# One decoder step with grouped experts: from pairs of tiles to a pipeline of single tiles, with seven pairs' rows picked by the tensor engine from on-chip tokens

## What is computed

```python
def _hier_moe(x, w_group, b_group, w_expert, b_expert, w1, w3, w2):
    ...
    global_idx = g_idx * EXPERTS_PER_GROUP + e_idx
    combine = jnp.sum(jax.nn.one_hot(global_idx, N_EXPERTS, dtype=jnp.float32)
                      * gate[..., None], axis=1)
    ...
    for e in range(N_EXPERTS):
        hdn = jax.nn.silu(xf @ w1[e]) * (xf @ w3[e])
        acc = acc + combine[:, e:e + 1] * (hdn @ w2[e])
    return acc.reshape(bsz, T, d)

# layer:  x = LN1(alpha * x + mixer);  f = hier_moe(x);  x = LN2(alpha * x + f)
```

## Time and profile before

| what | us |
|---|---|
| device time, median of 3 runs (lowest, highest) | 725.46 (722.87, 726.48) |
| device time of the profiled execution | 724.48 |
| span of its trace, from the first to the last instruction | 722.7 |
| PE busy | 609.7 (84%) |
| DVE busy | 306.5 (42%) |
| ACT busy | 181.7 (25%) |
| POOL busy | 158.3 (22%) |

### The profile page before, as it was taken

The page is one execution under the profiler, slowest core; times in us unless marked ns, Lnnn a source line. Parts: engine busy times, 40 slices in busy tenths (PEclk is TensorE's granted clock), DMA queues, the critical chain, the costliest instruction groups (busy, mean ns, idle before and its releaser), DMA issues.

```text
span 722.7 us, 10598 instructions
## 1 busy us (share of the span) xinstructions
PE 609.7 (84%) x4220; PEld 419.2 (58%) x4220; DVE 306.5 (42%) x786; ACT 181.7 (25%) x287; POOL 158.3 (22%) x181
## 2 busy tenths in 40 slices
PE   5999999999899899799799798987777776877852
PEld 5999999878765356456445445544443534444430
DVE  4561585426584134344434343353426232323532
ACT  4232323201211223232332232223223222313210
POOL 1000000000000413343323234234132322224231
PEclk9999999999899999999999989999999999999996
DMA  9943033842668799999999999999999999999930
GB/s 268 282 159 133 2 117 117 350 189 103 246 293 349 285 418 420 418 417 416 422 415 419 414 423 417 421 418 417 422 417 424 414 426 416 424 419 416 391 135 8
DMA packets 45754, 235.99 MB, mean 327 GB/s; under 512 B 13683, under 2 KB 18291, under 8 KB 28728
## 3 DMA queue, kind: packets, MB, share of 16 engines
q1 hardware_dynamic: 32303, 220.92, 75.3%
q0 software_dynamic: 12544, 11.71, 4.8%
q10 hardware_dynamic: 857, 2.67, 0.9%
HBM read 237.69 MB, written 30.20 MB: 371 GB/s over the span
## 4 chain that ended last, share of the span: by engine, by line
issue 36%; SPq 18%; DMA 17%; PE 16%; POOL 9%; DVE 2%; ACT 1%; POOLq 0%; DVEq 0%
SPq L403 12%; DMA tenth_block<-in_w 12%; PE ps L543 9%; SPq L407 5%; PE ps L702 3%; DMA prev<-first_outputs,final_row 2%; POOL out L1094 2%; POOL first_outputs L1082 2%; POOL out L1090 2%; POOL prev L1086 2%; PE ps L723 2%; DMA first_outputs<-ye,first_row 2%; SPq L453 1%; DMA xe_odd<-x_rows,pair_row 1%; PE ps L506 1%
## 5 line engine op out<-in xcount | busy, mean ns | idle before, releaser
L702 PE MATMUL ps<-blocks,ln 128*64 128x256 f32 x1952 | 229.3, 391 | 54.4 <-DMA blocks<-in_w 38.7
L702 PEld LDWEIGHTS ps<-blocks,ln 128*64 128x64 f32 x1952 | 154.5, 140 | 128.6 <-issue 61.8
L723 PE MATMUL ps<-blocks,hT 128*64 128x512 f32 x464 | 109.9, 617 | 9.6 <-DMA blocks<-in_w 8.8
L1086 POOL DMA_INDIRECT prev<-first_outputs,final_row x32 | 34.4, 1076 | 234.3 <-DMA first_outputs<-ye_more,first_row 110.6
L723 PEld LDWEIGHTS ps<-blocks,hT 128*64 128x64 f32 x464 | 33.5, 141 | 68.0 <-issue 53.5
L807 ACT ACTIVATE ln<-ps 128x512 f32<-128x512 f32 (+1 forms) x38 | 20.0, 572 | 113.1 <-PE ps L690 94.2
L1496 DVE COPY hT<-ps 128x256 f32<-128x256 f32 x33 | 13.9, 421 | 71.3 <-PE ps L711 71.3
L543 PE MATMUL ps<-xT_high,w_in_high 128*128 128x288 f32 x256 | 40.6, 300 | 2.9 <-ACT w_in_high L807 1.7
L990 ACT ACTIVATE std<-rstd,eps 128x1 f32<-128x1 f32 x32 | 9.4, 295 | 123.9 <-DVEq L1523 114.3
L948 ACT ACTIVATE silu<-ps 128x256 f32<-128x256 f32 x33 | 12.7, 384 | 109.9 <-PE ps L702 105.3
L1491 DVE SCALAR_TENSOR_TENSOR h_rows<-silu,slot_gate,ps 128x256 f32<-128x256 f32 x33 | 15.7, 477 | 57.7 <-PE ps L702 57.6
(11 more groups left out here) (233 smaller groups left out, 787.4 us busy)
## 6 DMA issues: line engine op xcount, KB each, us to landing
blocks<-in_w SPq DMA_DIRECT2D x86, 2048.0 KB
tenth_block<-in_w SPq DMA_DIRECT2D x9, 2048.0 KB
blocks<-in_w_in SPq DMA_DIRECT2D x3, 2048.0 KB, 10.8
blocks<-in_w_out SPq DMA_DIRECT2D x2, 2048.0 KB, 7.9
x_tok<-in_x_prompt SPq DMA_DIRECT2D x4, 512.0 KB, 5.2
blocks<-in_w_in SPq DMA_DIRECT2D x4, 512.0 KB, 10.6
first_outputs<-in_x_prompt SPq DMA_DIRECT2D x4, 512.0 KB, 8.6
x_rows<-x_tok ACTq DMA_DIRECT2D x4, 512.0 KB, 2.7
```

What stands on the lines that cost most here:

```text
L702: mm = pe.matmul(ps[64 * g:64 * g + 64, bank, 0:FH], x, w[:, k, g * FH:(g + 1) * FH], start=(k == 0), stop=(k == KD - 1))
L723: mm = pe.matmul(ps[64 * g:64 * g + 64, BY, :], hT[:, k % 2, k // 2 * SLOTS:(k // 2 + 1) * SLOTS], w[:, k, g * DH:(g + 1) * DH], start=(k ...
L1086: return g.indirect_dma_start(out=prev[w], out_offset=None, in_=first_rows[:, :], in_offset=rows_at(idx), bounds_check=last_row, oob_is_er ...
```

## The change

- **PE runs single tiles**, one down behind: for tile t w1 t, turn t-1, w3 t, down t-1. The last tiles (30 to 32) do their own turn and down at once (`STAGGERED`).
- **The order of the loads** follows: w1 t, w3 t, w2 t-1. There are nine blocks, used in turn; the tenth is gone, since `x_tok` is still read.
- **Seven pairs are picked on chip**: for m = 3, 5, ..., 15 (`PICKED`) DVE makes a 0/1 matrix (`make_hot`) and PE multiplies it with `x_tok` (`pick_pair`, 10 products of 512 columns); ACT copies the result to `xe_odd` (`keep_xe`). The other nine are fetched as before.
- **POOL's loop** over t becomes `send(t-2)`, `load(t-1)`, `store(t-1)`, and `fetch` only where the pair isn't picked.
- **DVE's loop** becomes `final(t-2)`, `keep_hT(t-1)`, `products(t)`, `add_y(t-1)`, and `make_hot`.
- **ACT's loop** becomes `spread(t-2)`, `silu_of(t)`, and after odd t the copies and fills.
- **The start**: the token table is computed before the second `fetch_first`, `order` is made before the other index tables, the filler products on PE (`keep_warm`) are 21 in another place and 2 instead of 12.

```diff
+STAGGERED = E - 2
 def order_of_loads():
...
-    for m in range(1, PAIRS):
-        tiles = [t for t in (2 * m, 2 * m + 1) if t != SHARED + 1]
-        loads += [(kind, t) for t in tiles for kind in ("w1", "w3")] + [("w2", t) for t in tiles]
+    for t in range(E + 1):
+        loads += [(kind, t) for kind in ("w1", "w3")]
+        loads += [("w2", s) for s in ([t - 1] if t < STAGGERED else [t - 1, t] if t == STAGGERED else [t]) if s >= 0]
+    return [(kind, t) for kind, t in loads if t != SHARED + 1]
...
+HOME = [n % EARLY_BLOCKS for n in range(len(LOADS))]
+PICKED = list(range(3, PAIRS, 2))
...
             def block_free(n):
...
+                kind, t = LOADS[n - EARLY_BLOCKS]
+                sp.wait_ge({"w1": h1_done, "w3": h_done, "w2": y_done}[kind], t + 2 if t == SHARED else t + 1)
...
+            for n in range(EARLY_BLOCKS, EARLY_BLOCKS + 2):
+                block_free(n)
+                load(n)
+            sp.wait_ge(order_ready, 1)
+            for n in range(EARLY_BLOCKS + 2, EARLY_BLOCKS + 4):
...
-            keep_warm(21)
+            pe.wait_ge(out_kept, NT + 3)
+            keep_warm(4)
+            route(NT - 2)
+            turn_x1(NT - 1)
+            keep_warm(2)
+            route(NT - 1)
+            keep_warm(15)
...
+            def pick_pair(m):
+                n = PICKED.index(m)
+                pe.wait_ge(hot_ready, n + 3)
+                pe.wait_ge(xe_kept, 2 * n + 2)
+                pe.wait_ge(y_filled, 2)
+                for g in range(2):
+                    for j in range(NT):
+                        mm = pe.matmul(ps[:, BX[g], :], hot[:, j, :], x_tok[:, j, g * DH:(g + 1) * DH],
+                                       start=(j == 0), stop=(j == NT - 1))
+                    mm.then_inc(fetched, 1)
...
-            def first_pair():
+            def first_tiles():
...
+                token_table()
+                fetch_first(1, lambda: turn_hidden(0))
+                down(*place("w2", 0), 0, lambda: turn_first(1))
                 pe.wait_ge(xeT_ready, 2)
+                into_hidden("w1", *place("w1", 1), 1, 1)
+                into_hidden("w3", *place("w3", 1), 1, 1)
+                pe.wait_ge(table_ready, 1)
                 turn_pair(1)
...
-            def pair(m):
-                a, b = 2 * m, 2 * m + 1
-                pe.wait_ge(xeT_ready, 2 * m + 2)
-                into_hidden("w1", *place("w1", a), a, 0)
-                into_hidden("w3", *place("w3", a), a, 0)
-                into_hidden("w1", *place("w1", b), b, 1)
-                turn_hidden(a)
-                into_hidden("w3", *place("w3", b), b, 1)
-                down(*place("w2", a), a)
-                turn_hidden(b)
-                turn_pair(m + 1)
-                down(*place("w2", b), b)
+            def tile(t):
+                if t % 2 == 0:
+                    pe.wait_ge(xeT_ready, t + 2)
+                into_hidden("w1", *place("w1", t), t, t % 2)
+                if t <= STAGGERED:
+                    turn_hidden(t - 1)
+                into_hidden("w3", *place("w3", t), t, t % 2)
+                if t % 2:
+                    turn_pair((t + 1) // 2)
+                if t <= STAGGERED:
+                    down(*place("w2", t - 1), t - 1)
+                if t % 2 == 0 and (t + 2) // 2 in PICKED:
+                    pick_pair((t + 2) // 2)
...
-            keep_warm(12)
+            keep_warm(2)
+            first_tiles()
+            for t in range(2, E + 1):
+                tile(t)
+                if t >= STAGGERED:
+                    turn_hidden(t)
+                    down(*place("w2", t), t, last_half if t == E else None)
...
+            for t in range(2, E):
+                if t % 2 and (t + 1) // 2 in PICKED:
+                    keep_xe((t + 1) // 2)
+                if t > 2:
+                    spread(t - 2)
+                silu_of(t)
+                if t % 2:
+                    keep_xeT((t + 1) // 2)
+                    fill_pair((t + 1) // 2)
+            spread(E - 2)
+            spread(E - 1)
             silu_of(E)
-            spread(E - 1)
             spread(E)
...
-            g.memset(cleared[:, :], 0.0).then_inc(prev_cleared, 1)
+            g.memset(xe_odd[:, :, :], 0.0).then_inc(prev_cleared, 1)
             pool.wait_ge(prev_cleared, 1)
             pool.wait_ge(x1_stored, 16 * NT)
             fetch(1)
+            g.memset(prev_mem[:, :, :], 0.0).then_inc(prev_cleared, 1)
+            fetch(2)
             pool.wait_ge(first_cleared, 16 * NT)
             store(0)
-            load(1)
-            fetch(2)
-            store(1)
-            load(2)
-            for t in range(2, E - 1):
-                store(t)
-                send(t - 1)
-                if t < E - 2:
-                    load(t + 1)
-                if t % 2 == 0 and t // 2 + 2 <= PAIRS:
+            pool.wait_ge(prev_cleared, 2)
+            for t in range(2, E):
+                if t > 2:
+                    send(t - 2)
+                load(t - 1)
+                store(t - 1)
+                if t % 2 == 0 and t // 2 + 2 <= PAIRS and t // 2 + 2 not in PICKED:
                     fetch(t // 2 + 2)
+            load(E - 1)
             store(E - 1)
-            load(E - 1)
             send(E - 2)
             load(E)
...
+            def make_hot(m):
+                dve.wait_ge(fetched, 2 * PICKED.index(m) + 2)
+                for i in range(2):
+                    slot, one = pick_at[:, 2 + i, :], pick_at[:, 4, i * NT:(i + 1) * NT]
+                    settled(v.scalar_tensor_tensor(slot, pick_at[:, 0, :], float(2 * m + i), pick_at[:, 1, :],
+                                                   ALU.is_equal, ALU.mult))
...
+            for t in range(2, STAGGERED + 1):
+                if t > 2:
+                    final(t - 2)
+                keep_hT(t - 1)
+                products(t)
+                add_y((t - 1) % YR, t - 1)
+                if t % 2 and (t + 3) // 2 in PICKED:
+                    make_hot((t + 3) // 2)
+            keep_hT(E - 2)
+            add_y((E - 2) % YR, E - 2)
+            final(E - 3)
+            products(E - 1)
+            keep_hT(E - 1)
+            add_y((E - 1) % YR, E - 1)
+            final(E - 2)
             final(E - 1)
             products(E)
```

More of the change, by code:

```diff
@@ L197, in block_at @@
         def block_at(b):
-            return tenth[:, :] if b == EARLY_BLOCKS else blocks[:, b, :]
+            return blocks[:, b, :]
         def in_block(b):
@@ L323, in build @@
         extra_ready, order_ready = sem("extra_ready"), sem("order_ready")
-        block_loaded = [sem(f"block_loaded{b}") for b in range(EARLY_BLOCKS + 1)]
+        block_loaded = [sem(f"block_loaded{b}") for b in range(EARLY_BLOCKS)]
         hot_ready = sem("hot_ready")
@@ L475, in _ @@
                 sp.dma_start(ln2[64 * g:64 * g + 64, 1, :], ln2_b[half].partition_broadcast(SLOTS)).then_inc(ln2_loaded, 16)
[L476 to L477 removed]
+            for n in range(EARLY_BLOCKS + 4, len(LOADS)):
                 block_free(n)
@@ L616, in turn_x1, with keep_warm @@
                         mm.then_inc(x1_turned, 1)
+            def keep_warm(products):
+                for _ in range(products):
+                    pe.matmul(ps[:, 2, 0:P], ident[:, :], ident[:, :], start=True, stop=True)
             def route(j):
@@ L639, in _ @@
                 turn_x1(j - 1)
-            for j in range(NT - 2, NT):
-                route(j)
-                if j + 1 < NT:
-                    turn_x1(j + 1)
-            def keep_warm(products):
-                for _ in range(products):
-                    pe.matmul(ps[:, 0, 0:P], ident[:, :], ident[:, :], start=True, stop=True)
-            keep_warm(21)
+            pe.wait_ge(out_kept, NT + 3)
[5 more added lines that the diff above has]
+            keep_warm(15)
             pe.wait_ge(mask_ready, 1)
@@ L669, in fetch_first @@
                 for j in range(NT):
+                    if before_last and j == NT - 1:
+                        before_last()
                     for g in range(2):
@@ L712, in turn_hidden, with down @@
                 mm.then_inc(h_turned, 1)
-            def down(b, loads, seq, last=False):
+            def down(b, loads, seq, halfway=None):
                 w = out_block(b)
@@ L719, in down @@
                 for k in range(KF):
-                    if last and k == KF // 2:
-                        pe.wait_ge(last_loaded, 16)
+                    if halfway and k == KF // 2:
+                        halfway()
                     for g in range(2):
@@ L1576, in _ @@
             dve.sem_inc(table_ready, 1)
+            add_y(0, 0)
             products(1)
-            add_y(0, 0)
-            keep_hT(1)
-            add_y(1, 1)
-            for m in range(1, PAIRS):
-                products(2 * m)
-                keep_hT(2 * m)
-                final(2 * m - 1)
-                products(2 * m + 1)
-                add_y(2 * m % YR, 2 * m)
-                keep_hT(2 * m + 1)
-                final(2 * m)
```

(3 more changed lines are left out.)

138 lines of the change are left out of this document (57 added, 81 removed).

## The result

| | us |
|---|---|
| kernel before, median of 4 runs beside it | 725.77 (722.87 to 726.48) |
| changed kernel, median of 4 runs | 777.79 (775.72 to 782.83) |
| ratio | 1.0735, interval 1.0676 to 1.0795 |
| span of the profiled execution after | 775.4 |

The change costs 52 us. The prediction said slower, by 22.5 us, for the reason that the trace then shows; the size lies outside its range.

The account below looks back on a forecast made before the run. It took POOL's queue order to make load, final and sends a serial ring that bounds the kernel: 246.4 + 461.1 + 38.7 = 746.2 us of span, plus 1.8 around it, 748.0 us; range 724 to 772.

Parts of the forecast that it names:

- issue of load 1: Start: store 0 goes at 238.4, takes 8.0 us, so POOL issues load 1 at 246.4; the start gives 3.2 us.
- P: Middle: period of one tile's serial turn, L + 7.5, taken as 15.9 us; 29 turns make 461 us.
- from load 30 to the end: End: store 30, load 31, final 31 and the kept last steps, 38.7 us in all.
- L: Time from a load's issue on POOL to the start of its final on DVE: taken as 8.4 us, ends 7.7 and 9.3.
- Rivals 1 and 2: First: weights stay the bound, about 716 us, 9%. Second: nothing changes, L of 7.6 gives the old time by chance, 5%.
- Rival 1: Weight stream stays the bound if L falls under about 7.0, for instance with gathers gone: about 716 us, 9%.
- 5 less: End in the weights-bound case: 24.1 us after the last landing shrink by 5, as `products` no longer waits for a final.
- Rival 4: PE sets the pace, through picks in every other tile and a half clock for stretches; needs 15.9 us a tile; 2%.
- rival 3: Loads get slower behind two sends, L from 9.3 on: 776 us, 17%; against it, idle DMA engines would lower L.
- What is hidden: Work said to cost no time: seven picks on PE at 4.5 us each, `make_hot`, ACT's table switches, saved gathers, tenth block.
- the ring: POOL and DVE: load, final, step and two sends run serially each tile, nothing overlapping; 15.2 to 16.6 us a tile, 67%.
- what would show it: Profile signs: `prev` waits 29 times, 200 us or more; loads 15 to 17 us apart; DMA share under 1 only at the end.

Follow-up runs that it names:

- e1: Changed kernel with load(t-1) ahead of send(t-2) in POOL's loop, picks kept: 742.50 us, ratio 1.0230.
- e4: Kernel before with only POOL's loop in the order of the change (send, load, store, fetch): 764.07 us, ratio 1.0534.
- e2: Changed kernel with no pair picked, all 16 pairs fetched from DRAM, POOL's order as in the change: 770.97 us, ratio 1.0654.
- e12: Changed kernel with only the fetch of pair 2 moved from ahead of store 0 to behind load 1: 776.23 us, ratio 1.0686.
- e6: Changed kernel with POOL's, DVE's and ACT's queues reordered to give slack between tiles, picks and nine blocks kept: 729.01 us, ratio 1.0028.
- e3: Changed kernel with load(t-1) ahead of send(t-2) on POOL and no pair picked: 740.42 us, ratio 1.0217.

## Why the prediction was right, and where it was wrong

The profiled span decomposes by the prediction's own terms:

| term | predicted | measured | difference |
|---|---|---|---|
| issue of load 1 | 246.4 | 250.8 | +4.4 |
| 29 turns of P | 461.1 (15.9) | 490.2 (16.90) | +29.1 |
| from load 30 to the end | 38.7 | 34.4 | -4.3 |
| span | 746.2 | 775.4 | +29.2 |

The two small differences, +4.4 and -4.3, cancel by luck.

**Right:** the mechanism and its form (P = L + final + step + two sends), what would be queued behind it, and the reading that the weights would no longer be last; e1 and e4 show it from both sides. Rivals 1 and 2 did not come. Rival 1's condition, L under 7.0, was met in none of the kernels whose L is given above. (Its "5 less" for `products` of the last tile is a misreading: the changed order keeps final 31 ahead of it.) Rival 4, PE at the pace, came in four turns only, those of tiles 7, 9, 28 and 29.

**The term that failed is the turn, P = L + 7.5.** Its parts over the 29 turns measured 8.81 + 5.12 + 0.28 + 2.69, against 8.4 + 4.6 + 0.3 + 2.6:

- *L, +0.41 a turn, 12 us.* I mixed the mean of before with the two loads that stood near sends, and put the new loads in between. No row of before had the new situation: there no load up to tile 31 stood less than 4.4 us behind a send (tiles 3 and 7, with 8.6 and 9.7: 5.6 and 6.7 us); now it is 1.3. My reading that only loads near sends are slow came from three rows; the loads of tiles 12, 16 and 18 took 9.0 to 9.2 us with the sends 9.6 to 11.7 us ahead. The mean of all 16 that DVE waited for was 8.11, not 8.05 over 15. The kernels with the load right behind two sends measure 8.75 (e4), 8.81 (changed) and 8.98 (e2). Counting only loads that DVE waited for, the changed kernel has 9.43 in 25, which is rival 3's figure. What brought the mean down to 8.81 is in part rival 3's own counter-argument, idle DMA engines: tile 7's load took at most 3.9 us in the pause at 350 us, and tile 9's at most 2.2 in a second, short one (share 0.07 from 389 to 391.4 us). Elsewhere the stream filled the longer tile.
- *The final, +0.52 a turn, 15 us.* "What is hidden" priced the picks at 4.5 us of PE beside other work. Two errors. A pick takes 8.8 us: `fetch_first` has two products side by side on 64 columns each, the pick fills 128 columns with one. The same 20 records, twice the time. The Trainium skill ("TensorEngine Tiling (Array Packing)", Theoretical Speedup) gives two such halves up to twice the rate, and the 4.51 against 8.85 us here agree. And ACT copies the picked rows ahead of `spread`, in order, so the final waits on DVE for a square root that waits on ACT for the pick on PE. In the timeline of PE, DVE, ACT for final 7:

```profile
356.52 8.85 PE L686 MATMUL ps<-x_tok,hot 128*128 128x512 f32 x20
356.70 0.69 DVE L1531 TENSOR_TENSOR ye_more<-ye_more,ps 128x512 f32<-128x512 f32 x1 [5.12 <-PE ps L733]
357.49 0.69 DVE L1537 TENSOR_TENSOR prev<-prev,ye_more 128x512 f32<-128x512 f32 x1
...
365.41 0.60 ACT L813 ACTIVATE xe_odd<-ps 128x512 f32<-128x512 f32 x1 [3.63 <-PE ps L686]
366.02 1.28 ACT L996 ACT_TABLE_LOAD   x1
367.32 0.29 ACT L996 ACTIVATE std<-rstd,eps 128x1 f32<-128x1 f32 x1
367.64 0.16 DVE L1555 RECIPROCAL rstd<-std 128x1 f32<-128x1 f32 x1 [6.40 <-ACT std L996]
```

  11.1 us for a final instead of 4.6, and on the ring. It is the worst of five: the finals of tiles 3, 7, 11, 19 and 27, each beside one of the seven picks, take 5.8 to 11.1 us, the other 24 take 4.6. Without picks (e2) the mean final is 4.60 again and P 16.55; L rose by 0.17 there, and the median is 7 us lower, which the overlapping intervals alone would not prove. I had priced an operation by its busy time on one engine and not asked which queue its consumer stands in, although the changed order showed the copy ahead of the square root.
- *Sends, +0.09 a turn, 3 us*, nearly all of it two loads, of tiles 10 and 29, that also waited for a store (1.7 and 1.9 us).

**Load 1, +4.4.** The issue of store 0, 238.4 predicted, was 236.86; its landing, taken from before as 8.0, took 13 us. The new order puts a 512 KB fetch 1.3 us ahead of it. The rows, POOL:

```profile
235.55 1.01 POOL L1118 DMA_INDIRECT ln<-x_rows,pair_row  x1 [3.52 <-ACT ye L978]
236.86 1.02 POOL L1096 DMA_INDIRECT first_outputs<-ye,first_row  x1 [0.30 <-issue]
250.82 1.04 POOL L1100 DMA_INDIRECT prev<-first_outputs,final_row  x1 [12.94 <-DMA first_outputs<-ye,first_row]
```

In e12, without that fetch ahead, the store landed within 3.6 us. But e12 doesn't show that the fetch alone cost the rest: its store (235.95) was nearly over when SP's next weight block went out (238.51; share 0.40 from 236 to 240 us), while here the block went out at 234.78, ahead of the store, and the share was 0.83 in these 4 us and 1.00 in the next 4. What an earlier load 1 would be worth is open; final 1 had another wait close behind. **The end, -4.3:** load 31 was issued 3.9 us behind load 30 and not 7.8, as store 30 landed fast once the stream was over.

**The range was too narrow.** It ended at 772, 4 us over the top of my own forecast and short of rival 3's 776, for which I had 17%. That 776 came nearest in time, in part by luck: its mean L of 9.3 did not come, and the longer finals (15 us), which it does not have, took the place of what L fell short (14 us). The picks' price, taken from one row of another shape, had no upper end in it at all.

**Signs in "what would show it" that failed.** DVE's wait for `prev` is 123.5 us in 25, not 200 or more in 29, since part of the 9 us of a load passes while DVE copies hT, makes `products` and waits for PE's down product (`ye` L1531 <- PE L733, 131.6 us in 30). Of the 28 distances from load 2 to load 30 only seven lie between 15 and 17 us. Four are under 15 (11.1, 14.6, 14.3 and 14.1), which by my own test would have meant that I am wrong; the first comes in the second pause of the stream and the last in a turn that PE held, so a single distance was a poor test and the mean, 16.9, a better one. The other signs came: POOL's largest wait, the late last store, PE without waits for blocks, the stream over 40 us before the end. I expected the DMA share under 1 only at the end. It fell to 0.13 from 350 to 370 us. The code says why: tiles 8 and 9 share one expert's blocks, and `block_free` frees them only after tile 9's products. SP stood 28.9 us until PE had done w1 of tile 9 (365.30 + 3.67 us) and issued the next block at 369.72. PE was late there, held by the ring and by the pick at 356.52. In e6, where the turns are shorter, there is no such pause.

## What to carry to other kernels

An in-order queue that issues load t behind send t-1 turns a chain of transfers and compute into one serial turn per tile; look at which tile the wait ahead of each load belongs to, and keep at least two tiles between them on every queue that the chain passes (here POOL, DVE and ACT; mending one left a second ring over two tiles). Work moved to another engine has its price where its result is copied, in the queue of the consumer; price it by a row of the same tile shape. And a bound that is full (a share of 1.01) is worth no transfer saved until nothing slower runs beside it: the same picks gave 5.2 us where the stream was the limit, and none with the ring (the medians say a loss of 7 us, with intervals that overlap).

## What the runs showed of the hardware that was not expected

- A load of 128 rows of 2 KB on POOL's queue took from 5.9 to 12.4 us in the changed kernel from its issue to the final that waited for it, nearly always beside a weight stream of about 418 GB/s, and at most 2.2 us in a pause of the stream (share 0.07). With two sends issued directly ahead it took longer: 9.58 against 8.20 us on average at the same share of 1.01 (e2 and e3, 400 to 650 us).
- The store of tile 0, 128 rows of 2 KB, landed 13 us after its issue, 1.3 us behind a 512 KB gather on the same queue and beside the weight stream, and within 3.6 us with no gather right ahead and the stream just about to go on (235.95 to 239.56 in e12). Which of the two costs the 9 us is not shown.
- A product with 128 stationary columns took twice the time of two with 64 each side by side (8.85 against 4.51 us for 20 records, both at a granted clock of 1.00).
